# Decay and gate rows on 32 partitions each, a reordered beginning, and VectorE makes the low parts of the value blocks

## The reference

```python
m_lat = silu(c) @ mod_w[0] + mod_b[0]            # shift, scale, gate (and m_ctx from c_ctx)
u  = rms_norm(h,  norm_mix_w) * (1 + sc1) + sh1  # uc likewise from the context
z = u @ w_in                                     # gq gk gv gg | ga | mq mk mv mo | mg
gq, gk, mq, mk = rope(...)                       # latent tokens only
a_pre = einsum('btzr,zre->zbte', ga, a_up) + a_bias     # z: forward, backward; rank 16
log_a = log_sigmoid(a_pre) / 16
b = cumsum(log_a, within chunks of 64 tokens)
q_dec, k_dec = q * exp(b), k * exp(-b)
log_i, log_f = mg + bias, log_sigmoid(mg + bias)        # 4 heads, 2 directions
```

## Time and profile before

| | before |
|---|---|
| median of 3 runs (lowest to highest) | 1690.18 us (1689.37 to 1691.69) |
| profiled execution: time | 1691.74 us |
| its span, first to last instruction | 1689.9 us |
| TensorE busy | 1650.0 us, 98% |
| VectorE busy | 1130.8 us, 67% |
| ScalarE busy | 898.5 us, 53% |
| GpSimd busy | 675.4 us, 40% |
| mean granted TensorE clock | 0.989 of full |

### The profile page before, as it was taken

How to read it: one execution, slowest core, us unless ns; L and a number is a source line. 1 busy time by engine, 2 the same in 40 slices (tenths; PEclk the granted TensorE clock), 3 DMA queues, 4 the chain that set the end, 5 groups by cost and what they waited for, 6 DMA issues and landing times.

```text
span 1689.9 us, 27413 instructions
## 1 busy us (share of the span) xinstructions
PE 1650.0 (98%) x10098; PEld 1457.3 (86%) x10098; DVE 1130.8 (67%) x1807; ACT 898.5 (53%) x1529; POOL 675.4 (40%) x494
## 2 busy tenths in 40 slices
PE   8999999998999999999999999999999999999997
PEld 5777888887899999999888889987668989999886
DVE  4587966666978888888657664145773788886113
ACT  5673435776465555655333453214884557776322
POOL 2144225453234444444443533332005266665444
PEclk9999999999999999999999999999999999999998
DMA  9432224343212233233733333364214123232221
GB/s 360 141 120 98 83 76 150 102 143 119 75 63 76 83 102 93 93 104 103 287 129 121 125 110 127 125 220 151 85 59 148 51 92 109 100 100 102 100 90 61
DMA packets 71240, 197.43 MB, mean 117 GB/s; under 512 B 6322, under 2 KB 27186, under 8 KB 69826
## 3 DMA queue, kind: packets, MB, share of 16 engines
q1 hardware_dynamic: 49268, 177.29, 30.2%
q10 hardware_dynamic: 21840, 18.40, 3.6%
HBM read 187.22 MB, written 8.45 MB: 116 GB/s over the span
## 4 chain that ended last, share of the span: by engine, by line
PE 75%; DVE 12%; ACT 7%; issue 2%; DMA 2%; POOL 2%; ACTq 0%; DVEq 0%; SPq 0%; POOLq 0%
PE ps L3821 18%; PE ps L3332 8%; PE ps L3319 7%; PE ps L3956 7%; PE ps L4024 6%; PE ps L3444 4%; PE ps L3953 3%; PE ps L3318 3%; PE ps L3771 2%; PE ps L4124 2%; PE ps L4137 2%; PE ps L4103 2%; PE ps L3894 2%; DMA raw<-in_weights 1%; PE ps L3450 1%
## 5 line engine op out<-in xcount | busy, mean ns | idle before, releaser
L892 POOL TENSOR_TENSOR wsp<-raw,wsp 128x512 fp32r<-128x512 f32 x220 | 328.5, 1513 | 687.5 <-ACT wsp L1045 687.2
L1045 ACT ACTIVATE wsp<-raw 128x1024 fp32r<-128x1024 f32 x110 | 116.7, 1061 | 173.8 <-PE ps L3319 85.0
L3956 PE MATMUL ps<-hsp,wsp 128*128 128x512 f32 x456 | 154.8, 392 | 0.0
L3821 PE MATMUL ps<-T,wun 128*128 128x384 f32 (+1 forms) x792 | 148.9, 341 | 3.9 <-DVE ps L2221 2.7
L3821 PEld LDWEIGHTS ps<-T,wun 128*128 128x128 f32 x792 | 141.6, 190 | 4.8 <-issue 3.7
L3332 PE MATMUL ps<-wsp,u 128*128 128x512 f32 x576 | 132.5, 390 | 0.8 <-PE ps L3332 0.6
L3332 PEld LDWEIGHTS ps<-wsp,u 128*128 128x128 f32 x576 | 107.6, 188 | 25.2 <-issue 2.8
L3319 PE MATMUL ps<-u,wsp 128*128 128x512 f32 (+1 forms) x384 | 126.3, 365 | 0.0
L3444 PE MATMUL ps<-u,wsp 128*128 128x512 f32 x384 | 122.7, 401 | 0.0
L3953 PE MATMUL ps<-hsp,wsp 128*128 128x256 f32 x432 | 119.8, 281 | 1.6 <-DVE hsp L2821 1.0
L4024 PE MATMUL ps<-hsp,wsp 128*128 128x512 f32 x480 | 110.9, 390 | 1.8 <-POOL wsp L892 1.8
(11 more groups left out here) (412 smaller groups left out, 3888.1 us busy)
## 6 DMA issues: line engine op xcount, KB each, us to landing
raw<-in_weights SPq DMA_DIRECT2D x281, 512.0 KB, 3.3
nab<-in_nabias ACTq DMA_DIRECT2D x32, 256.0 KB, 2.7
start_w<-in_start SPq DMA_DIRECT2D x6, 1024.0 KB, 20.9
hidden_scratch<-hid0a SPq DMA_DIRECT2D x16, 384.0 KB, 4.6
hid0a<-hidden_scratch SPq DMA_DIRECT2D x5, 768.0 KB, 6.6
h<-in_x SPq DMA_DIRECT2D x4, 768.0 KB, 7.6
mD<-rows_scratch ACTq DMA_DIRECT2D x12, 256.0 KB, 4.0
mqs<-rows_scratch ACTq DMA_DIRECT2D x12, 256.0 KB, 5.2
```

The costliest lines, as they stand in the source:

```text
L892: pool.tensor_tensor(w[:, 1, half], raw[:, raw_index(s) % 4, half], w[:, 0, half].bitcast(F32), ALU.subtract)\
L1045: act.activation(split_of(s)[:, 0, :], raw[:, raw_s % 4, :], ACT.Copy).then_inc(*own.one(hi_ready))
L3821: mm = pe.matmul(out, UNIT[x][:, wp, tile(i)], operand[:, i, xp, 0:out.shape[-1]], start=(start and i == 0 and a == 0), stop=(i == KH - 1 ...
L3956: mm = pe.matmul(lat_of(layer, g, mm_), w, hsp[:, kk, xp, LAT], start=one, stop=last, skip_group_check=True)
```

## The change

On TensorE the decay products are made for both directions at a time, on partitions 0 to 31 and 32 to 63 of `small` (`decay_pair(p)`), the gate rows on 64 to 95 and 96 to 127, and they stand at other places between blocks 3 and 4; ScalarE takes them in another order. In the beginning the spread of `rt` comes before quarter 0's rows, row copies come between the decayed feature rows on ScalarE, VectorE scales four rows before quarter 0's columns, and two transfers change places. The first logs move behind `evict(4)` on ScalarE. VectorE makes the low parts of the eight value blocks (`value_low`, one instruction of 1024 columns), GpSimd skips them, and `turned`, `modulate` and `decayed` change places with them. The matmuls of the large products are the same.

```diff
@@ -816,7 +816,10 @@
             load(raw_index(0))
-            for q in range(1, START_Q):
+            load_quarter(1, 0)
+            load_quarter(1, 1)
+            load(raw_index(1))
+            for q in range(2, START_Q):
                 load(raw_index(q))
@@ -896,7 +899,11 @@
             pool.memset(mv[:, :, :, ML_DH:ML_DH + 1], 1.0).then_inc(*own.one(ones_ready))
-            for s in range(N_START, s_feat(P2_FIRST) + 2):
+            for s in range(N_START, S_V):
+                low(s, 0)
+            lo_ready.k += N_V
+            pool.wait_ge(lo_ready.sem, s_count(S_V + N_V - 1, 0))
+            for s in range(S_V + N_V, s_feat(P2_FIRST) + 2):
                 low(s, 0)
@@ -1275,17 +1282,18 @@
             row_taken(0)
-            high(1)
             first_row(0)
             first_high(0)
+            high(1)
+            row_taken(1)
             first_row(1)
             first_high(1)
-            row_taken(1)
             high(2)
-            for k in (2, 3):
-                first_row(k)
-                first_high(k)
+            first_row(2)
+            first_high(2)
             row_taken(2)
+            first_row(3)
+            first_high(3)
             for k in (4, 5):
@@ -1309,8 +1317,8 @@
-                b = 3 + 2 * (zp % 2)
-                act.wait_ge(apre_done.sem, zp + 1)
+                b = 3 + 2 * (zp // 2)
+                act.wait_ge(apre_done.sem, zp % 2 + 1)
                 for t, bank, w in ((LAT, b, N_LAT), (CTX, b + 1, N_CTX)):
@@ -1324,7 +1332,7 @@
-                act.wait_ge(rows_done.sem, 2)
+                act.wait_ge(rows_done.sem, 1)
                 for row, b, col in ((rA, 3, 0), (rB, 5, 1)):
@@ -1389,15 +1397,15 @@
             evict(1)
+            evict(2)
             decay_taken(0)
-            evict(2)
+            decay_taken(2)
+            evict(3)
             decay_taken(1)
-            decay_taken(2)
-            decay_logs((0, 1))
             decay_taken(3)
-            evict(3)
             rows_evict()
             evict(4)
+            decay_logs((0, 1))
@@ -1408,11 +1416,11 @@
                 if b <= 1:
+                    act.wait_ge(block_used.sem, S_V + b + 1)
+                    high(S_V + b + 2)
                     if b == 0:
                         decay_logs((2, 3))
-                    act.wait_ge(block_used.sem, S_V + b + 1)
-                    high(S_V + b + 2)
-                    if b == 1:
+                    else:
                         decay_exps(0)
@@ -2341,15 +2349,14 @@
             dve.wait_ge(norm_spread.sem, norm[0].turn)
-            row_scaled(0)
+            for k in range(4):
+                row_scaled(k)
             quarter_columns(0)
-            for k in range(1, 4):
-                row_scaled(k)
-            first_low(0)
             row_scaled(4)
             row_scaled(5)
+            first_low(0)
+            row_scaled(6)
             first_low(1)
-            row_scaled(6)
             row_scaled(7)
@@ -2395,6 +2402,15 @@
+            def value_low(b):
+
+                s = S_V + b
+                w = split_of(s)
+                dve.wait_ge(lo_ready.sem, s_count(s - 1, 0))
+                dve.wait_ge(hi_ready.sem, s_count(s, 0))
+                dve.tensor_tensor(w[:, 1, :], raw[:, raw_index(s) % 4, :], w[:, 0, :].bitcast(F32), ALU.subtract)\
+                   .then_inc(lo_ready.sem, 1)
+
             modulate(0, 0)
@@ -2403,11 +2419,13 @@
             modulate(4, 0)
+            turned(3)
             modulate(S_V, 0)
+            value_low(0)
+            turned(4)
+            value_low(1)
             running_sum(0)
             running_sum(1)
-            turned(3)
-            turned(4)
@@ -2482,21 +2500,22 @@
                     modulate(S_V + b + 1, 0)
-                elif b == 2:
-                    modulate(S_V + 3, 0)
-                    for zp in range(2):
-                        decayed(zp)
-                elif b > 3 and b % 4 != 3:
+                elif b > 3:
                     modulate(S_V + b, 0)
...
                     running_sum(2)
+                    value_low(2)
                     running_sum(3)
+                elif b in (1, 2):
+                    value_low(b + 2)
                 if b == 4:
...
                     dve.memset(gS[:, :, 0, :, :], 0.0).then_inc(*own.one(state_zero))
+                    value_low(6)
                 if b == 5:
                     rows_sums()
+                    value_low(7)
                     rows_gains()
@@ -2507,11 +2526,13 @@
                     dve.tensor_copy(out, src).then_inc(*own.one(v_dve))
+                    if b == 3 and i < 4:
+                        decayed(i // 2)
                 if b == 3:
-                    for zp in range(2, 4):
-                        decayed(zp)
-                else:
                     modulate(S_V + b, 0)
+                    decayed(2)
+                    value_low(5)
+                    decayed(3)
@@ -3379,6 +3400,8 @@
                 pe.wait_ge(start_rows.sem, CCOL_READY + q + 1)
+                if q:
+                    pe.wait_ge(t_ready.sem, 2 * q)
                 for t in range(4):
@@ -3399,14 +3422,14 @@
-            quarter_rows(0)
             pe.wait_ge(ident_loaded.sem, 16)
...
             mm.then_inc(*own.one(norm_spread))
+            quarter_rows(0)
             quarter_turned(0)
-            kept_warm(5)
+            kept_warm(3)
             quarter_rows(1)
@@ -3416,14 +3439,14 @@
             first_row(2, 0)
+            first_row(2, 1)
             quarter_turned(2)
-            first_row(2, 1)
             for b in range(3):
...
             first_row(0, 3)
+            first_row(1, 3)
             quarter_turned(3)
-            first_row(1, 3)
             first_row(2, 3)
@@ -3471,37 +3494,38 @@
-            def decay_inputs(zp):
-                b = 3 + 2 * (zp % 2)
-                if zp >= 2:
-                    pe.wait_ge(apre_taken.sem, 2 * (zp - 1))
-                elif zp == 1:
+            def decay_pair(p):
+
+                if p == 0:
                     pe.wait_ge(in_act_took.sem, 3)
                     pe.wait_ge(in_dve_took.sem, 2)
-                for t, bank, w in ((LAT, b, N_LAT), (CTX, b + 1, N_CTX)):
-                    mm = pe.matmul(ps[:, bank, 0:w], aup[:, zp // 2, tile(zp % 2)], small[:, t], start=True, stop=True)
+                else:
+                    pe.wait_ge(apre_taken.sem, 4)
+                for x, (t, w) in enumerate(((LAT, N_LAT), (CTX, N_CTX))):
+                    for z in range(2):
+                        rows = slice(32 * z, 32 * z + 32)
+                        mm = pe.matmul(ps[:, 3 + 2 * z + x, 0:w], aup[rows, z, tile(p)], small[rows, t], start=True, stop=True)
                 mm.then_inc(*own.one(apre_done))
...
             first_row(2, 6)
+            first_row(2, 7)
+            projection(3, range(5))
             pe.wait_ge(const_loaded.sem, 16 * 5)
-            pe.wait_ge(in_act_took.sem, 1)
-            decay_inputs(0)
-            first_row(2, 7)
-            projection(3, range(4))
-            decay_inputs(1)
-            decay_inputs(2)
-            projection(3, range(4, KT))
-            decay_inputs(3)
-            projection(4, range(4))
+            decay_pair(0)
+            projection(3, range(5, KT))
+            projection(4, range(2))
+            decay_pair(1)
+            projection(4, range(2, 6))
             pe.wait_ge(apre_taken.sem, 8)
-            for c, b in ((0, 3), (1, 5)):
-                for t, bank, w in ((LAT, b, N_LAT), (CTX, b + 1, N_CTX)):
-                    mm = pe.matmul(ps[0:64, bank, 0:w], sel[:, c, :], small[:, t], start=True, stop=True)
-                mm.then_inc(*own.one(rows_done))
-            projection(4, range(4, KT))
+            for x, (t, w) in enumerate(((LAT, N_LAT), (CTX, N_CTX))):
+                for c in range(2):
+                    rows = slice(64 + 32 * c, 96 + 32 * c)
+                    mm = pe.matmul(ps[0:64, 3 + 2 * c + x, 0:w], sel[rows, c, :], small[rows, t], start=True, stop=True)
+            mm.then_inc(*own.one(rows_done))
+            projection(4, range(6, KT))
```

## The result

| | before | after |
|---|---|---|
| 12 runs each, taken together: median | 1691.2 us | 1699.32 us |
| lowest to highest | 1686.97 to 1695.71 | 1690.89 to 1700.56 |
| mean | 1691.11 | 1697.88 |
| profiled execution: time (span) | 1691.74 (1689.9) | 1700.24 (1698.3) |

The changed kernel is slower: ratio 1.004, 95% interval 1.003 to 1.0051, some 6.8 us by the means. In one and the same kernel the single runs lie up to 10 us apart.

What follows compares the result with a forecast made beforehand. It took TensorE, nearly always busy, as the bound: its waits, clock and own work. Opening -4.1, decay and gate rows -3.2 and value stage +11.05 sum to +3.75 on 1690.18, so 1693.9 us, range 1688 to 1699.

Steps and rivals of the forecast that it cites:

- Opening, -4.1: 18 to 66.5 us: reordered start removes a wait and half clock, adds 1.1 and 0.5 us of waits; net -4.1 us.
- The stall on `start_row`: TensorE's 2.1 us wait on ScalarE's row copy 2, 38.6 to 40.67 us, was to go.
- Rival 1: Opening: the clock falls there too, near 34 us, costing about 3.4 us, 1697.3 in total; chance 0.2.
- Rival 3: Opening gains nothing, its stall moving whole to block 1's low part: +4.1 us, 1698.0 in total; chance 0.12.
- the 3.4 us of half clock: Opening: TensorE's loss at half clock after the 2.1 us wait, counted as going away with that wait.
- Decay and gate rows, -3.2: 66.5 to 94.2 us: twelve products run in overlapping pairs, -3.35 us; with waits and restarts the stage gains 3.2 us.
- The wait before block 3: Between blocks 0 and 3: TensorE, with less work in between, waits 1.85 us for VectorE to take block 1.
- Rival 2: Decay and gate products: pairs on different 32 partitions don't overlap, +3.35 us, 1697.3 in total; chance 0.07.
- the 0.07 us on top of a group's columns: Decay and gate products: each of three groups was taken as 1.28 us for 768 columns plus 0.07, 4.05 in all.
- Value stage, +11.05: After block 4: 0.3 us on tile 0, 7.6 standing still before block 7, 2.7 half clock, 0.45 at block 10.
- Rival 4: Value stage: log chain shorter without two table loads per group, wait 2.5 us, 1686.1 in total; chance 0.16.
- The half clock behind the wait: Value stage: TensorE's clock drops after standing still 7.6 us before block 7, costing 2.7 us, ends 1.7 and 3.4.

Runs made afterwards that it cites:

- the second experiment: Changed kernel with block 7's low part moved behind running_sum(0), plus decay and gate products reading all 128 partitions: 1700.96 us, ratio 1.0055 to the kernel before.

## Why the prediction was right, and where its sizes were off

The forecast was 1693.9 and slower; slower it is, by nearly twice as much (+6.8 by the means, +3.75 forecast). The median, 1699.32, lies at the upper end of the range of 1688 to 1699, 0.3 us beyond it. At the mark the first pair of profiles is nearer, +4.4, and part of that is luck: the opening and the decay stage gained 0.7 and 0.6 less than forecast, the value stage lost 0.65 less.

**Opening, -4.1; measured -3.4.** Block 0's result is copied 3.4 us earlier than in the first profile of before, both with a long start. The stall on `start_row` is gone, as is the half clock. GpSimd's low part made TensorE wait 0.6 us (1.1 forecast), row copy 3 another 0.6 (0.5). The first product came at 30.24, not 30.0; the rest of the 0.7 us by which it missed I can't assign. Rival 1, a fall of the clock near 34, was in none of the nine profiles of the changed opening. Rival 3's mechanism, the stall moving whole to block 1's low part, is out too: that wait is 0.6 us. Its price, no gain from the opening, is not excluded by the runs of the opening alone (0.7 slower to 3.7 faster). The mis-sized term is the 3.4 us of half clock. It was read from one profile and counted as always there, and in one profile of four it was not. With three in four it is 2.6 us on average, so the opening gains 2.6, not 3.4, and the change costs 0.8 more than one pair of profiles shows: like for like +4.2 at the mark against the profiles of before with the fall, +7.7 against the one without, +5.1 on average. It also gives the opening alone -3.1 and the idle products on the kernel before -2.3, both inside what their runs allow, neither confirmed by them. A rarer fall fits the runs better: were it there in one execution of four, the same sums would give -1.4 for the opening alone (measured -1.5), -0.6 for the idle products (-0.8) and +6.8 for the change (+6.8). That the granted clock differs from one execution to the next is shown; how often it falls is only guessed, from four profiles.

**Decay and gate rows, -3.2; measured -2.6.** Three groups of 1.56, 1.56 and 1.51 us for 7.4 before: -2.8. I had 4.05 us for them, it is 4.6. The wait before block 3 is 1.7 (forecast 1.85). Rival 2 is refuted by the second experiment: on all rows the same groups cost some 3.0 us more, 3.35 was written. The mis-sized term is the 0.07 us on top of a group's columns. A group of four products (two of 512 columns, two of 256) lasts 1.56 us, and the columns of one pair alone are 1.28 (from 768 at the earlier trace rows's pace): 0.28 and not 0.07. The change of tile shape does show. A group on 32 rows starts 0.32 us after the start of the product of 512 columns before it (71.23, then 71.55, and so at all three groups); on all rows it is 0.23 (70.41, then 70.64, in the second experiment). That is 0.09 us at each way in, 0.3 in all. What the way out costs can't be read apart from the group's own time. Block 4 is done at 88.3, 1.4 later than forecast.

**Value stage, +11.05; measured +10.4.** Counted from block 4's end, the chain held to the microsecond: `value_low(2)` ends 24.0 us after it (forecast 24.7), TensorE stands still 7.0 (7.6), tile 0 waits 0.62 (0.6), block 10 0.3 (0.45). That is the mechanism named, shown by three experiments: moved ahead of the logs the low part no longer stops block 7, made by GpSimd it doesn't either, and with both early the stage has no such wait. Rival 4, a chain short by the table loads, did not happen: ScalarE's groups start 9.45 us apart, each with both loads of 1.28.

The half clock behind the wait was the other size that was off. It lasted as long as before (109.2 to 116.0), but began while TensorE stood still: only the 3.65 us from 112.35 to 116.0 were worked at half clock, which costs 1.8 (1.6 by the idle products). What I had not counted: `modulate` of block 12 moved ahead of VectorE's last copies. One of its instructions takes 2.12 us for 1.2 while GpSimd runs (157.78 to 161.83), and three copies run in a row at the end:

```profile
160.79 2.12 DVE L2073 SCALAR_TENSOR_TENSOR left<-raw,c_both 128x1024 f32<-128x1024 f32 x1
...
164.17 2.28 DVE L2528 COPY mv<-ps 128x512 f32<-128x512 f32 x3
```

The last wait is 1.5 for 0.8: +0.7, and putting the modulation back took exactly that off. Waits and clock together: 7.0 + 0.3 + 1.8 + 0.3 + 0.7 = 10.1 of the 10.4.

**Behind the mark.** The profiles of the changed kernel are at +8.0 and +5.9 by 1660 us, the second one of before at +1.4. The clock also falls between 384 and 402 us in all 14 profiles, for 6.8 us in eight and 3.4 in six, and near 480 us in some executions and not in others, and waits for data come and go. Of the 6.8 us by the means 5.1 are at the mark if the fall in the opening of before comes three times in four; the other 1.7 then lie in what differs between executions or in something the change does further on. If the fall is rarer, as the runs suggest above, nothing is left. Two profiles of the changed kernel and four of before can't tell these apart, and it stays open.

## What to carry to other kernels

When work is given to another engine, its cost is where it stands in that engine's list: a 1.2 us instruction cost 7 us of wait, and 1.8 more by the clock, because it was written behind a chain of logarithms that it does not need; two low parts moved ahead took some 8 us off the slower kernel, which was then as fast as the one before, and with one more move faster. Follow such a move one need further: after block 7's low part was moved, block 8's was late for the same reason. And a clock loss behind a short gap, read from one profile, is one draw: profile the kernel again before you count it as a term.

## What the runs showed of the hardware that was not expected

- A wait of 2.1 us with a light product behind it dropped TensorE's granted clock to 0.5 in three of four profiled executions of one kernel, for 6.8 to 6.9 us, and not in the other. A wait of 2.2 us in front of small products dropped it in the one profile that had it, for 3.4 us; waits of 1.5 us at the same place did not in six. Waits of 4.2 and 7.0 us with heavy work on both sides dropped it in all four profiles that had them.
- Idle products of 256 columns through a wait kept the clock at 1.00 and made the kernel 5.4 to 5.7 us faster by the ratios, where the profiles explain 1.6 to 1.8. I have no reason for the rest.
- The stretch of half clock at the start was 6.8 us long in 6 of the 14 profiles and 3.4 in 8, which alone moves all that follows by some 1.3 us.
- Going from products on 128 rows to pairs on 32 rows put 0.09 us between the last large product and the first small one, at all three places.
